# A gated recurrence on one core: chunks of 16 with a carried state against one triangle built from tree levels

## The reference, cut to what matters

```python
z = u @ w_in[l]
hq, hf, hi, hg, aq, ak, av, iq, ik, iw, ga, gb = split_cols(z, IN_SIZES)
y_h = hgrn2_mix(hq, hf, hi, hg, lbs[l], hgrn_norm_w[l])
y_a = dsa_mix(aq, ak, av, iq, rmsnorm(ik, idx_k_norm_w[l]), iw, topk)
m = (sigmoid(ga) * (y_h @ w_branch_hgrn[l]) + sigmoid(gb) * (y_a @ w_branch_dsa[l]))
```

```python
diff = b[:, :, :, None, :] - b[:, :, None, :, :]
A = einsum('bhtd,bhtsd,bhsd->bhts', qc, exp(where(mask, diff, -inf)), kcc)
o = einsum('bhtd,bhde->bhte', qc * exp(b), S) + einsum('bhts,bhse->bhte', A, vc)
S = exp(b_last)[..., None] * S + einsum('bhsd,bhse->bhde', kcc * exp(b_last - b), vc)
```

## Time and profile before

| | |
|---|---|
| three runs | 1748.84, 1751.43, 1752.01 us (median 1751.43) |
| the profiled execution | 1753.83 us, span 1752.2 us |
| PE, share of the span | 1711.5 us, 98% |
| PE weight loads | 1610.0 us, 92% |
| DVE | 1063.4 us, 61% |
| ACT | 740.1 us, 42% |
| POOL | 90.4 us, 5% |
| chain that ended last | PE 91%, DVE 4%, issue 2%, ACT 1%, DMA 1% |
| TensorE's mean granted clock | 0.993 |
| from HBM | 283.66 MB, 166 GB/s over the span |

### The profile page before, as it was taken

How to read it: one execution, slowest core, us unless ns; L and a number is a source line. 1 busy time by engine, 2 the same in 40 slices (tenths; PEclk the granted TensorE clock), 3 DMA queues, 4 the chain that set the end, 5 groups by cost and what they waited for, 6 DMA issues and landing times.

```text
span 1752.2 us, 32506 instructions
## 1 busy us (share of the span) xinstructions
PE 1711.5 (98%) x12835; PEld 1610.0 (92%) x12835; DVE 1063.4 (61%) x1441; ACT 740.1 (42%) x798; POOL 90.4 (5%) x186
## 2 busy tenths in 40 slices
PE   6999999999999999999999999999999999999998
PEld 5989998889889999789999999999988999999886
DVE  4454597766755555677655566666544666666453
ACT  6333354444422232456544444554433344344342
POOL 0000010000010011110123200000000000000000
PEclk9999999999999999999999999999999999999999
DMA  6654455545543434135765555565455555555652
GB/s 198 172 157 141 135 167 186 162 156 167 162 143 108 146 97 131 63 114 172 237 215 172 187 178 174 186 192 192 165 195 180 185 188 192 189 176 171 217 194 84
DMA packets 249281, 291.04 MB, mean 166 GB/s; under 512 B 9745, under 2 KB 235506, under 8 KB 248818
## 3 DMA queue, kind: packets, MB, share of 16 engines
q1 hardware_dynamic: 242434, 279.45, 49.2%
q0 software_dynamic: 2176, 6.46, 1.1%
q10 hardware_dynamic: 4608, 4.23, 0.7%
HBM read 283.66 MB, written 6.32 MB: 166 GB/s over the span
## 4 chain that ended last, share of the span: by engine, by line
PE 91%; DVE 4%; issue 2%; ACT 1%; DMA 1%; SPq 0%; ACTq 0%; DVEq 0%
PE ps L597 24%; PE ps L598 22%; PE ps L599 22%; PE ps L909 5%; PE ps L908 5%; PE ps L906 5%; PE ps L722 2%; PE ps L700 2%; PE ps L674 1%; PE ps L727 1%; DVE w_lo L1228 1%; ACT w_hi L950 1%; DMA raw<-in_w_in_dram 1%; PE ps L640 0%; DVE score L1313 0%
## 5 line engine op out<-in xcount | busy, mean ns | idle before, releaser
L597 PE MATMUL ps<-u_hi,w_hi 128*128 128x258 f32 (+2 forms) x2976 | 863.1, 290 | 6.6 <-DVE z_v L1340 2.5
L599 PE MATMUL ps<-u_hi,w_lo 128*128 128x258 f32 (+2 forms) x2976 | 848.3, 285 | 0.0
L598 PE MATMUL ps<-u_lo,w_hi 128*128 128x258 f32 (+2 forms) x2976 | 848.3, 285 | 0.0
L1228 DVE TENSOR_TENSOR w_lo<-raw,w_hi 128x2048 fp32r<-128x2048 f32 x262 | 602.8, 2301 | 303.1 <-ACT w_hi L950 303.0
L950 ACT ACTIVATE w_hi<-raw 128x2048 fp32r<-128x2048 f32 x262 | 501.5, 1914 | 514.6 <-PE ps L599 328.3
L597 PEld LDWEIGHTS ps<-u_hi,w_hi 128*128 128x128 f32 x2976 | 565.3, 190 | 25.0 <-issue 14.9
L598 PEld LDWEIGHTS ps<-u_lo,w_hi 128*128 128x128 f32 x2976 | 565.9, 190 | 0.1
L599 PEld LDWEIGHTS ps<-u_hi,w_lo 128*128 128x128 f32 x2976 | 565.4, 190 | 0.0
L906 PE MATMUL ps<-w_hi,hid_hi 128*128 128x512 f32 x352 | 137.8, 391 | 0.0
L909 PE MATMUL ps<-w_lo,hid_hi 128*128 128x512 f32 x352 | 137.1, 389 | 0.0
L908 PE MATMUL ps<-w_hi,hid_lo 128*128 128x512 f32 x352 | 137.0, 389 | 0.0
(11 more groups left out here) (245 smaller groups left out, 1526.8 us busy)
## 6 DMA issues: line engine op xcount, KB each, us to landing
raw<-in_w_in_dram SPq DMA_DIRECT2D x48, 2048.0 KB, 8.5
raw<-in_w_ffn_gate_dram SPq DMA_DIRECT2D x22, 2048.0 KB, 8.0
raw<-in_w_ffn_up_dram SPq DMA_DIRECT2D x22, 2048.0 KB, 8.0
raw<-in_w_ffn_down_dram SPq DMA_DIRECT2D x20, 2048.0 KB, 7.7
raw<-in_w_out_dram SPq DMA_DIRECT2D x8, 2048.0 KB, 8.9
raw<-in_w_branch_hgrn_dram SPq DMA_DIRECT2D x8, 1024.0 KB, 5.5
raw<-in_w_branch_dsa_dram SPq DMA_DIRECT2D x8, 1024.0 KB, 8.4
gate_spill<-gate_st ACTq DMA_DIRECT2D x32, 129.0 KB, 1.8
```

What stands on the lines that cost most here:

```text
L597: mm(acc, w_hi[s][:, k, :], mov_hi(k), start=(k == first), stop=False)
L598: mm(acc, w_hi[s][:, k, :], mov_lo(k), start=False, stop=False)
L599: ins = mm(acc, w_lo[s][:, k, :], mov_hi(k), start=False, stop=(k == last))
L1228: v.tensor_tensor(w_lo[m % 4][:], raw[(m // 2) % 2][:, :, P * (m % 2):P * (m % 2) + P], w_hi[m % 4][:].bitcast(F32), ALU.subtract).then_in ...
```

## The change

The recurrence loses its chunks, its state and its chain of steps. The 256 tokens after the meta tokens are treated as one triangle of token pairs, split as a binary tree splits it: at level l (block m = 2^l, l = 0 to 7) the queries of the second half of each block of 2m tokens meet the keys of the first half. `logs` holds running sums of the logarithms within blocks of m, so that key and query side each get one exponential whose argument is never positive. For a level DVE subtracts (`spans`), ACT takes two exponentials (`level_decays`), DVE multiplies by keys and queries (`weigh`) and doubles the block of the running sums (`sum_up`), PE computes 8 products of 128 x 128 (`grams`), and DVE copies their valid entries under a mask (`take_level`). The second 128 tokens lie reversed, so that one product of a level serves both halves of the sequence. Diagonal, meta tokens and values follow as single jobs (`diagonal`, `meta_pairs`, `meta_grams`, `turn_v`, `outputs`). All of it lies beside the 32 gate units, which are written out (no loop): a level takes two units, `weigh` in the even one, `grams` after the fourth of 16 row blocks of the odd one.

POOL builds the masks (31 operations from L501 on, each waiting for the one before) in place of clearing the band and the staging tiles. The 24 attention units have only eight sums of squares beside them, their square roots and reciprocals included. The first 8 query units and the first 8 attention units (queries) take 258 columns. The scores of two indexer heads are computed together, once in two units. Keys in unit 4 of the values take three DVE operations a head instead of two, the value copies two instead of one.

```diff
-            sp.wait_ge(band_zeroed, 1)
-            sp.wait_ge(band_taken, 5)
-            for j in range(4):
-                sp.dma_start(band[32 * j:32 * j + CH, :, :].rearrange("s (a j) t -> s j a t", j=4)[:, j, :, :],
-                             band_rows[:].rearrange("s (a j) t -> s j a t", j=4)[:, j, :, :])\
-                    .then_inc(band_spread, 16)
...
+            steps.link(pool, pool.memset(masks[:], 1.0))
+            steps.link(pool, pool.memset(anti[:], 0.0))
...
+            for level in range(7):
+                m = 1 << level
+                first, second = (masks[:, level, 64 * a:64 * a + 64].rearrange("p (n i) -> p n i", i=m)
+                                 for a in range(2))
+                up, down = [[2 * m, 64 // m], [0, m]], [[-2 * m, 64 // m], [0, m]]
+                keep_where(first, down, 0, 1)
+                keep_where(first, up, m - 1, -1)
+                keep_where(second, down, P - 1, -1)
+                keep_where(second, up, m - P, 1, True)
+            pool.wait_ge(chosen, 2)
+            pool.memset(intra[0][:], 0.0).then_inc(intra_zeroed, 1)
+            pool.wait_ge(forget_ready, 1)
+            pool.memset(intra[1][:], 0.0).then_inc(intra_zeroed, 1)
...
+                    if u % 2 == 0:
+                        pe.wait_ge(iq_staged, 2 * i + (u // 2 + 1))
+                        pe.wait_ge(relu_done, 8 * i + (2 * u + 4))
+                        for t in range(2):
+                            for b in range(2):
+                                half = slice(64 * b, 64 * b + 64)
+                                ins = mm(ps[2 + 2 * b + t][:, 0:T], iq_st[u // 2][half, P * t:P * t + P], ki[half, :],
+                                         start=True, stop=True)
+                                if t == 1:
+                                    ins.then_inc(scored, 1)
                     n = U_QFI + u
                     pe.wait_ge(z_free, 4 * i + (n + 1))
-                    project(4 * i + n, n % 4, n % 2, 0)
+                    project(4 * i + n, n % 4, n % 2, t0)
+            with pe.Fori(0, 2) as i:
+                query_forget(i, T0)
+            with pe.Fori(2, 4) as i:
+                query_forget(i, 0)
...
+            def grams(level):
+                pe.wait_ge(x_made, 3 * level + 3)
...
+                for h in range(HEADS):
+                    ins = mm(ps[2 + 2 * (level % 2) + h // 4][:, P * (h % 4):P * (h % 4) + P],
+                             xs[level % 2][:, 0, h, :], xs[level % 2][:, 1, h, :], start=True, stop=True)
+                ins.then_inc(gram_done, 1)
...
+                mm(o[:, 0:TQ], v_tok[h % 2][0:CH, 2, :], intra_meta[:, h, :], start=True, stop=False,
+                   skip_group_check=True)
+                mm(o[:, 2:TQ], v_tok[h % 2][:, 0, :], part[:, h % 4, 0::2, :], start=False, stop=False,
+                   skip_group_check=True)
+                mm(o[:, 2 + P:TQ], v_tok[h % 2][:, 1, :], part[:, h % 4, 1, :], start=False, stop=True,
+                   skip_group_check=True).then_inc(o_made, 1)
...
+            def gate_jobs(u):
+                jobs = []
+                if u < 16 and u % 2:
+                    jobs.append((4, lambda: grams(u // 2)))
+                if u in (16, 18):
+                    jobs.append((4, lambda: diagonal((u - 16) // 2)))
+                if u in (18, 19):
+                    jobs.append((10, lambda: meta_grams(u - 18)))
+                if u == 20:
+                    jobs.append((4, meta_pairs))
+                if 21 <= u < 29:
+                    jobs.append((2, lambda: turn_v(u - 21)))
+                if 22 <= u < 30:
+                    jobs.append((10, lambda: outputs(u - 22)))
+                return jobs
...
-                    for s in (2 * u, 2 * u + 1):
-                        pe.wait_ge(pair_ready, 16 * i + (s + 1))
-                        for a in range(2):
-                            o = ps[2 + a][0:CH, 0:T].rearrange("p (c t) -> p c t", t=CH)[:, :, s:CH]
-                            r = pairs[s % 2][:, NC * a:NC * a + NC, s:CH]
-                            ins = mm(o, onehot[:, 15 - s:31 - s], r, start=(s == 0), stop=(s == CH - 1))
-                        ins.then_inc(band_used, 1)
...
-                mm(o, kv_tok[:, 1, :], a_st[slot][:, h0:h0 + 4, :].rearrange("p h t -> p (h t)"),
-                   start=True, stop=False, skip_group_check=True)
-                for j in range(4):
-                    ins = mm(o[:, CH * j:CH * j + CH], state[:, h0 + j, :], q_st[slot][:, h0 + j, :],
-                             start=False, stop=True, skip_group_check=True)
-                if update:
-                    for j in range(4):
-                        tok = slice(32 * j, 32 * j + CH)
-                        ins = mm(ps[UPDATE_BANKS[j]][:, 0:P], kv_tok[tok, 0, :], kv_tok[tok, 1, :],
-                                 start=True, stop=True)
-                ins.then_inc(step_done, 1)
...
+                pe.wait_ge(z_free, n - 32 + 1)
+                with_jobs(n, T0 if u < 8 else 0, [(8, lambda: o_squares(u // 3))] if u % 3 == 1 else [])
...
+                activation(x[:, 0, :, :], x[:, 0, :, :], ACT.Exp).then_inc(decay_ready, 1)
+                if level < 7:
...
-                        v.tensor_scalar(z_k[:, h, :], z_k[:, h, :], lb[:, 3, h:h + 1], None, ALU.mult)
+                        v.tensor_scalar(z_k[:, h, 0:END], k_sig[:, h, 0:END], lb[:, 3, h:h + 1], None, ALU.mult)
+                        v.tensor_scalar(z_k[:, h, T - 1:END - 1:-1], k_sig[:, h, END:T], lb[:, 3, h:h + 1], None,
+                                        ALU.mult)
...
-                if u == 6:
-                    dve.wait_ge(log_ready, 1)
-                    for h in range(HEADS):
-                        ins = v.tensor_tensor_scan(z_b[:, h, :], keep[:], z_b[:, h, :], 0.0, ALU.mult, ALU.add)
-                    link(ins)
...
-                v.tensor_copy(z_v[:, u, :], ps[m % 2][:, 0:T]).then_inc(z_free, 1)
...
+                v.tensor_copy(z_v[:, u, 0:END], ps[m % 2][:, 0:END])
+                v.tensor_copy(z_v[:, u, T - 1:END - 1:-1], ps[m % 2][:, END:T]).then_inc(z_free, 1)
...
+                    for a, out in ((0, x[:, 0, :, :]), (1, x[:, 0, :, ::-1])):
+                        c = halves(logs[:, :, META + P * a:META + P * a + P], m)
+                        v.tensor_tensor(halves(out, m)[:, :, :, 0, :],
+                                        c[:, :, :, 0, m - 1:m].to_broadcast([P, HEADS, 64 // m, m]), c[:, :, :, 0, :],
+                                        ALU.subtract).then_inc(span_ready, 1)
...
+                        xk = halves(x[:, 0, :, :], m)[:, :, :, a, :]
+                        v.tensor_tensor(xk, xk, halves(z_k[:, :, META + P * a:META + P * a + P], m)[:, :, :, a, :],
+                                        ALU.mult).then_inc(x_made, 1)
...
+                    v.tensor_tensor(xq, xq, halves(z_q[:, :, META:T], m)[:, :, :, 1, :], ALU.mult).then_inc(x_made, 1)
...
+                v.tensor_tensor(c[:, :, :, 1, :], c[:, :, :, 1, :],
+                                c[:, :, :, 0, m - 1:m].to_broadcast([P, HEADS, n, m]), ALU.add).then_inc(summed, 1)
...
+                    v.copy_predicated(halves(intra[g][:, :, 0:2, :].rearrange("p h a t -> p h (a t)"), m)[:, :, :, 1, :],
+                                      masks[:, level:level + 1, :].bitcast(mybir.dt.int32)
+                                      .rearrange("p a (n m) -> p a n m", m=m).to_broadcast([P, 4, P // m, m]),
+                                      ps[2 + 2 * (level % 2) + g][:].rearrange("p (h n m) -> p h n m", h=4, m=m))\
+                        .then_inc(gram_taken, 1)
...
+                    weigh(u // 2)
+                    sum_up(u // 2)
+                if u < 14 and u % 2:
+                    take_level(u // 2)
```

More of the change, by code:

```diff
@@ L34 @@
 CH = 16
-NC = T // CH
 IDXH = 16
@@ L520, in _, with keep_where @@
-            for c in range(2):
-                stage(c, c)
-            with pool.Fori(1, 8) as i:
-                for b in range(2):
-                    pool.wait_ge(step_done, 4 * i + (2 * b - 2))
-                    stage(2 * i + b, b)
-            pool.wait_ge(step_done, 2 * (NC - 1) - 2)
-            stage(NC - 1, (NC - 1) % 2)
+            def keep_where(tile, pattern, base, cm, last=False):
+                ins = pool.affine_select(out=tile, in_=tile, compare_op=ALU.is_ge, fill=0.0, base=base,
+                                         pattern=pattern, channel_multiplier=cm)
+                if last:
+                    ins.then_inc(masks_made, 1)
+                else:
+                    steps.link(pool, ins)
```

520 lines of the change are left out of this document (259 added, 261 removed).

## The result

The changed kernel takes 1655.17 us (median of four runs, 1653.48 to 1658.42); the kernel before took 1751.72 beside it. The profiled executions are 1753.83 and 1656.06 us, a saving of 97.8 where the forecast had 78.6.

What follows compares the result with a forecast made beforehand. The prediction took PE's order of matmuls as the bound; its terms (-13.2 + 4.6 + 3.4 + 3.1 - 67.7 - 10.5 + 1.7) summed to -78.6 us, giving a forecast of 1673 us, range 1661 to 1694.

Steps and rivals of the forecast that it cites:

- Queries, forget gates, scores: Score stage: paired 64-row score products overlap, saving 10.5 us, and 14 columns less in eight units save 2.7; sum -13.2.
- 0.40 is left for entering and leaving a job: PE's jobs between projections: beyond its records, each job costs 0.40 us, read from a score job of 1.31 us.
- The waits in the gate stage and the last gate copy: Gate stage: PE waits 0.75 us for operands at each level, 6.0 in all, and 1.0 for the last copy.
- Values: Value units: PE waits behind DVE's copies, delayed by 24 forget gate operations that meet POOL's mask selects; +4.6 us.
- One wait of about 6 us: Sign in the values: PE idles once for about 6 us, behind forget gate operations stretched by POOL.
- The clock: PE's clock falls after idle gaps: +3.4 us behind the wait in the values, +1.7 behind the tail, half of 3.4.
- Attention stage and tail: Attention projections fall from 216.8 to 149.1 us, -67.7; the tail from 12.6 to 2.1 us, -10.5.
- Rival 1: Masks late: POOL's 31 chained operations are held up by `w_lo`, DVE waits before its first level; 1686 us, 7%.
- Rival 2: Score stage: the 64-row products of the scores don't overlap; +7.4 us, 1680 us, 6%.
- Rival 3: Gate stage: DVE is slow on every second word at level 0; +6.1, 1679 us, 17%; every level, 1713, 3%.
- the forecast's dear case: Gate stage: two masked copies on DVE take 2.6 us at the scan's 2.5 ns an element, instead of 1.4.
- Rival 4: Gate stage: each level's waits keep PE's clock at 1.2 GHz; 1781 us with 16 units, 1886 with all 32; 1%.

Runs made afterwards that it cites:

- the repeat: The changed kernel run once more with no edit: 1653.81 us, 0.9445 of the kernel before.
- scores apart: Changed kernel with only the pairing of the score products undone, one head at a time, 258 columns kept: 1665.80 us, 0.9510 of the kernel before.
- masks early: Changed kernel with POOL building the level masks ahead of the two bias selects, no other edit: 1651.88 us, 0.9434 of the kernel before.

## Why the prediction was wrong, step by step

- **Queries, forget gates, scores** (-13.2, measured -12.9): right, each of its two parts by an experiment of its own.
- **"0.40 is left for entering and leaving a job"** is the step that failed. The number was right for the job that it was read from and was carried to jobs of another form. It belongs to products that fill 64 rows; full ones cost their records alone. That makes eight `grams` and two `diagonal` jobs 1.78 us instead of 2.16 (-3.8) and eight sums of squares 0.45 instead of 0.83 (-3.0), which is all but 0.1 of the miss in the attention stage. These 6.8 us are the largest part of the miss, and the range had no room for them: its lower end let the meeting with POOL, the falls of the clock and the levels' waits go, but kept this price. All jobs of the gate stage together cost 221.5 - 182.8 = 38.7 us, forecast 43.2.
- **The waits in the gate stage and the last gate copy** (6.0 + 1.0, measured 226.3 - 221.5 = 4.8): the place and the cause were right, the operands were 0.2 us earlier than reckoned and level 0 had none. "PE waiting under 1 us at each `x_made`" held.
- **Values** (+4.6, measured +1.3): too dear by the bare operation (0.30 for 0.24) and by the meetings. "One wait of about 6 us" was 3.47.
- **The clock** (+3.4 and +1.7): the first was 6.8, 3.4 or 0 us of the lower level, hence 2.6 us in the first profile and nothing in the repeat. Of nine profiles with the 2.0 us gap in the tail, one (scores apart) had it fall behind that, for 3.4 us, which cost 1.5. The forecast charged the first in full and half of the second, so it put one value on something that happens in part of the executions.
- **Ahead of the scores** (0, measured -2.7) and **behind the tail** (0, -0.9): the first is the clock's rise, which the profile of before had late. The sum was made against that profile's own time, and only 2.4 us of its distance to the median were taken off. The second lies with the first attention head, and the forecast had no term for it. Before, PE had a step of 0.88 us ahead of that head's turned probabilities, 0.76 above an ordinary one: the softmax began 1.20 us after the start of the last logits product, behind a reciprocal of the recurrence. In the changed kernel it begins 0.24 us after it, there is no such gap, and the stage of the attention heads is 0.8 us shorter. This is read from the two traces, no run tried it:

```profile
727.76 0.27 PE L782 MATMUL ps<-ident,probs 128*16 128x128 f32 x1 [0.60 <-DVE probs L1453]
```

- **Attention stage and tail** otherwise as forecast: no step of the recurrence is left there, no two starts of PE inside the stage lie over 0.32 us apart, so the written-out code stopped it nowhere, and the tail is one gap of 2.0 us. The forecast's parts of that gap (0.33, 0.44 and 1.12) add up to 1.9, not to its 2.1, and 1.9 is what the gap has above an ordinary step.

Rival 1, masks late, did not come: the selects ended at 241.96 us, and VectorE's first level, which waits for them, began at 249.60 without an idle before it. They were held up, though: 17.36 us for 28. Rival 2 is settled by the scores apart. Rival 3, slow single words at level 0, shows in no subtraction and no product. In the changed kernel level 0 multiplies and copies at 254.51 and 260.81, level 1 at 268.35 and 274.16, and both levels read alike (starts apart, a product takes 0.61 and a masked copy 1.12 us):

```profile
254.51 1.30 DVE L1407 TENSOR_TENSOR xs<-xs,z_qf 128x512 f32<-128x512 f32 x2 [1.10 <-ACT xs L1080]
...
260.81 2.49 DVE L1429 COPY_PREDICATED intra<-masks,ps 128x512 f32<-128x512 int32 x2
...
268.35 1.29 DVE L1407 TENSOR_TENSOR xs<-xs,z_qf 128x512 f32<-128x512 f32 x2
...
274.16 2.48 DVE L1429 COPY_PREDICATED intra<-masks,ps 128x512 f32<-128x512 int32 x2
```

The Trainium skill (Vector Engine (DVE) Microarchitecture Reference, Measured stream behaviour on trn2) gives 1.7 to 2.5 ns for an element in single words. An estimate from that is 0.87 to 1.28 us at level 0 for one of these two products of 512; the pair of them takes 1.30 us at level 0 and 1.29 at level 1. The measurement decides: for `tensor_tensor`, every second word costs nothing here. The masked copies are slow at levels 0 and 1, two in 2.5 us as in the forecast's dear case and in 1.3 us above, and the slack covered them, as the forecast said. Rival 4, the clock low in the gate stage, had no part; PEclk was 1.00.

## What to carry to other kernels

Read the price of a job from a job with the same shape: one entry cost 0.41 us for products of 64 rows and nothing for products of 128. Where one execution's profile is the base of a sum, look at when its clock rises and falls first, and set these terms apart as drawn. A wait that several instructions of another engine share (both banks free, all copies done) is worth splitting, but the gain counts only if the next thing in the chain is early too: of the 2.0 us in the tail, 1.3 came back at the next wait until one chain on VectorE was moved.

## What the runs showed of the hardware that was not expected

- A change of the rows that a matmul fills, there and back, costs 0.41 us between full ones; no change costs nothing, however often a job is cut (24 cuts: 0.0 us).
- TensorE's clock first rises at one of two times, 26.9 to 28.6 or 35.3 to 36.0 us, in executions whose instructions up to there are alike, and that is worth some 3 us. Behind the same idle gap of 3.47 us it was low for 6.8, 3.4 or 0 us. Behind gaps of 0.95 to 1.99 us in the same place, four profiles, it never fell; among the chunk steps of the kernel before, gaps of 1.84 and 2.00 us each came with a fall (from 499.5 and 509.8 us on, 3.4 us each). So the length of a gap alone doesn't tell.
- A masked copy out of PSUM of 128 x 512 takes 1.31 to 1.38 us where its runs are one or two words (levels 0 and 1), and 0.69 to 0.74 at the levels with longer runs. `tensor_tensor` of the same size shows no such difference between level 0 and the others.
- Writing backwards costs VectorE nothing that shows. With masks early, where GpSimd does nothing beside them, 128 elements written backwards take 0.28 us and 0.20 between starts, 144 forwards 0.29 and 0.21. (The 0.16 in the row at 223.81 stands behind an operation that was held up.)
